# Output projection joined to the turn by quarters, and the low parts of its first weights moved into the turn

## The reference

```python
mixed = jnp.concatenate([out_a, out_b], axis=-1)     # 256 tokens x 1024 features
return mixed @ w_out                                 # 1024 x 1024
# then x = x + norm(...) or x = x + gate * (...), and a feed-forward block or a mixture of experts follows
```

## Time and profile before

| | |
|---|---|
| time, median of 3 runs | 2291.13 us (2288.84 to 2291.92) |
| the profiled execution | 2288.96 us, span 2287.2 us |
| PE busy | 2098.6 us, 92% of the span |
| DVE busy | 1351.0 us, 59% |
| ACT busy | 1133.3 us, 50% |
| mean granted PE clock | 0.946 of 2.4 GHz |

### The profile page before, as it was taken

How to read it: one execution, slowest core, us unless ns; L and a number is a source line. 1 busy time by engine, 2 the same in 40 slices (tenths; PEclk the granted TensorE clock), 3 DMA queues, 4 the chain that set the end, 5 groups by cost and what they waited for, 6 DMA issues and landing times.

```text
span 2287.2 us, 31360 instructions
## 1 busy us (share of the span) xinstructions
PE 2098.6 (92%) x13218; PEld 1826.9 (80%) x13218; DVE 1351.0 (59%) x1302; ACT 1133.3 (50%) x1455; POOL 443.4 (19%) x305
## 2 busy tenths in 40 slices
PE   7998977999899899699999877999998986999997
PEld 6898967999899898699988666777777875877775
DVE  5766436556656584655653656566665247565665
ACT  4765445565566354456533534554443244454553
POOL 2683000474176100037510000000000000000000
PEclk9999988999999899799999988999998787999999
DMA  9897514787688463378754105878886203688874
GB/s 326 289 313 234 173 56 146 241 284 242 219 287 277 148 172 124 117 245 279 260 172 151 52 11 201 295 284 323 330 303 211 88 1 147 239 314 313 322 291 177
DMA packets 224348, 494.95 MB, mean 216 GB/s; under 512 B 11848, under 2 KB 167608, under 8 KB 199472
## 3 DMA queue, kind: packets, MB, share of 16 engines
q1 hardware_dynamic: 200608, 410.20, 52.3%
q0 software_dynamic: 23328, 81.71, 10.5%
q10 hardware_dynamic: 272, 1.05, 0.1%
HBM read 485.53 MB, written 12.10 MB: 218 GB/s over the span
## 4 chain that ended last, share of the span: by engine, by line
PE 82%; DVE 9%; ACT 3%; DMA 3%; issue 2%; POOL 0%; DVEq 0%; SPq 0%; ACTq 0%
PE psum L997 80%; DVE nrm L2069 2%; DMA big<-in_ada_w 2%; DVE low L2069 1%; DMA ring<-in_ffn_w_up 1%; PE psum L1063 1%; PE psum L1596 1%; ACT wh L1685 1%; PE psum L1240 1%; DVE xl L2069 1%; DVE wide L2069 0%; DMA ring<-in_moe_w_gate 0%; DVE nrm L2189 0%; DVE x L2392 0%; DVE nrm L2163 0%
## 5 line engine op out<-in xcount | busy, mean ns | idle before, releaser
L2069 DVE TENSOR_TENSOR low<-ring,wh 128x2048 fp32r<-128x2048 f32 (+2 forms) x338 | 811.3, 2416 | 532.0 <-ACT wh L1685 530.7
L1685 ACT ACTIVATE wh<-ring 128x2048 fp32r<-128x2048 f32 (+2 forms) x338 | 640.6, 1902 | 436.9 <-PE psum L997 236.8
L997 PE MATMUL psum<-xh,wh 128*128 128x256 f32 x1832 | 520.7, 284 | 13.4 <-DVE xl L2069 7.2
L997 PE MATMUL psum<-xl,wh 128*128 128x256 f32 x1832 | 520.0, 284 | 0.0
L997 PE MATMUL psum<-xh,low 128*128 128x256 f32 x1832 | 517.7, 283 | 0.0
L997 PEld LDWEIGHTS psum<-xh,wh 128*128 128x128 f32 x1832 | 352.1, 192 | 19.2 <-issue 15.5
L997 PEld LDWEIGHTS psum<-xl,wh 128*128 128x128 f32 x1832 | 350.1, 191 | 1.4
L997 PEld LDWEIGHTS psum<-xh,low 128*128 128x128 f32 x1832 | 350.5, 191 | 0.0
L769 POOL TENSOR_TENSOR big<-big 128x1024 f32<-128x1024 f32 x144 | 302.7, 2102 | 241.3 <-ACT big L1781 233.3
L997 PE MATMUL psum<-wh,xh 128*128 128x256 f32 (+5 forms) x864 | 278.6, 322 | 10.4 <-DVEq L667 5.9
L997 PE MATMUL psum<-wh,xl 128*128 128x256 f32 (+5 forms) x864 | 277.7, 321 | 0.0
(11 more groups left out here) (350 smaller groups left out, 2389.3 us busy)
## 6 DMA issues: line engine op xcount, KB each, us to landing
ring<-in_moe_w_gate SPq DMA_DIRECT2D x64, 1024.0 KB, 5.4
ring<-in_moe_w_up SPq DMA_DIRECT2D x64, 1024.0 KB, 6.0
ring<-in_moe_w_down SPq DMA_DIRECT2D x64, 1024.0 KB, 5.4
big<-in_ada_w POOLq DMA_DIRECT2D x48, 1024.0 KB, 6.7
ring<-in_ffn_w_gate SPq DMA_DIRECT2D x44, 1024.0 KB, 6.2
ring<-in_ffn_w_up SPq DMA_DIRECT2D x44, 1024.0 KB, 5.9
ring<-in_ffn_w_down SPq DMA_DIRECT2D x44, 1024.0 KB, 5.2
ring<-in_mlstm_w_in SPq DMA_DIRECT2D x16, 1024.0 KB, 5.6
```

Source lines behind the costliest of these rows:

```text
L997: return pe.matmul(out_, lhsT, rhs, start=start, stop=stop, **kw)
L1685: act.activation(wh[n % PARTS][:, 0:w], ring[SLOT_OF[n]][:, 0:w], ACT.Copy).then_inc(high, 1)
L2069: return dve.tensor_tensor(out_, a, b, op)
```

## The change

Outproj is joined to the turn ahead of it: the boundary between them is gone on all three engines. In its place PE waits, in the first piece alone, ahead of each run of 12 matmuls for the quarter of `xl` that it reads. On DVE the early low parts leave the mixer. One of them stands at the head of the turn, ahead of the four subtractions of `xl`; the second, where there was one, is made in outproj, behind the four. The high parts stay where they were.

```diff
@@ JOINED
-                                                         ("ffn", "setup"),
+                                                         ("ffn", "setup"), ("outproj", "turn"),
@@ PE, outproj
                     for t in range(TT):
                         for kt in range(KT):
+                            if j == 0 and kt % 4 == 0:
+                                pe.wait_ge(turn_low, 4 * ran(s, "turn") - 4 + 2 * t + kt // 4 + 1)
                             last = three(psum[:, 2 * t + j // 2, (j % 2) * 256:(j % 2 + 1) * 256],
@@ DVE, turn
                 if by_columns(s - 1):
                     return turn_columns(s, k)
+                if STAGES[s + 1][0] == "outproj" and early(s + 1):
+                    low_part(s + 1, PIECE0[s + 1], GU)
                 for q in range(4):
@@ DVE, outproj
             def outproj(s, k):
-                for j in range(len(early(s)), 4):
+                for j in range(min(1, len(early(s))), 4):
                     low_part(s, PIECE0[s] + j, GU)
@@ DVE, soft_attention
                     if i + 2 < len(run):
                         biased_scores(*run[i + 2])
-                    if i == len(run) - 1:
-                        for j, shape in enumerate(early(s + 2)):
-                            low_part(s + 2, PIECE0[s + 2] + j, shape)
                     if p == SOFT[name]["pairs"] - 1:
                         scaled_values(name)
@@ DVE, mlstm
-                for j, shape in enumerate(early(s + 2)):
-                    low_part(s, PIECE0[s] + j, shape)
                 dve.wait_ge(ml_act, 2 * H)
```

## The result

The changed kernel took 2277.05 us in the median of six runs (2273.09 to 2283.62), the kernel before 2290.25 (2280.44 to 2294.06). The ratio is 0.9945, with a 95% interval of 0.9926 to 0.9963: 0.55% faster, 13 us. Two later series of the same kernel gave 0.9921 (0.9905 to 0.9938) and 0.9943 (0.9924 to 0.9961), so some 15 us over the three. The prediction was 2274, with 2268 to 2283 as its range.

A forecast was written before the change was run, and what follows sets the result against it. PE, with 82% of the chain, was taken to bound the kernel. Mixer ends 8.2, boundary 6.1 and clock 3.0 us sum to 17.3, which from the 2291.13 us median gives 2274 us, rounded (range 2268 to 2283).

The forecast's parts named there:

- Low parts out of the mixer's end: At the four mixer ends, taking DVE's low parts away gives back 0.8, 2.35, 2.05 and 3.05 us, together 8.2.
- The low part inside the turn: At the turn's head, in DVE's idle time, it costs DVE's last result nothing; without that cover, 2.28 us a place.
- The boundary: Between turn and outproj, PE's first product starts right behind its transposes, needing only the first quarter: 6.1 us (5.6 to 6.6).
- The thin margin: In outproj, the second piece's low part is ready only 0.5 us before PE wants it, at one place 0.7.
- The clock: In outproj, unbroken work from the transposes on raises PE's clock sooner: +3 us of the 6.0 lost there.
- I see nothing that takes it back: In the stages behind outproj, joined and bound by PE, nothing takes back the 17.3 us gain.
- the waiting terms: At mixer ends and turns, the gains from shorter waits, 8.2 and 6.1 us, together 14.3.
- the waits go, the clock stays as it is: Rival, chance 0.27: in outproj the clock does not improve, only 14.3 us come back, time 2277 (2274 to 2280).
- The slower rival: Rival, chance 0.03: PE stays at 1.2 GHz through outproj; all four places slow to the end give 2315.

The follow-up runs named there:

- the single wait: Changed kernel with PE waiting once, ahead of its first product, for all four quarters, still without the boundary; 0.9931 and 0.9940 against the kernel before.
- the move alone: Kernel before with low parts moved as in the change, boundary between turn and outproj kept, no waits for quarters; 0.9965 and 0.9978 against the kernel before.

## Why the prediction was right, point by point

**Low parts out of the mixer's end: right.** 0.8, 2.35, 2.05 and 3.05 us were forecast. The three traces gave 0.69; 2.33, 2.35 and 2.29; 1.99, 1.84 and 1.99; and 2.98: 7.9 to 8.0 us for 8.2. What is late next was also as named: at A, C and D PE's last products, 0.1 us ahead of DVE's first write, and at B ACT's squares.

**The low part inside the turn: right,** and now shown from both sides: one at the head costs nothing, one without cover costs 4 us, and two at the head cost 2. The 2.28 us that were forecast for a lost cover were too few: they count from the fourth `xl`, which PE no longer waits for.

**The boundary: right in kind, mis-sized.** The term was 6.1 us with 6.6 as its upper end; it measured 7.1. I took PE to begin its products near the modelled end of its transposes, T0 + 3.6; it begins them at T0 + 3.14 to 3.33, some 0.3 us ahead of that end, right behind the start of the last one. The crossing itself costs next to nothing: with one wait for all quarters and no boundary the first product stands at 5.18, with the boundary at 5.13. The thin margin held: at C the second piece's low part ends at T0 + 8.2 and PE comes to that piece at T0 + 9.0, at A it is 8.4 and 9.2.

**The clock: right at the places, wrong beyond them.** I took +3 of 6.0 us. Outproj got 4.3 to 4.8 us shorter. Transposes alone bring the clock back: with the single wait no product had run before T0 + 5, and outproj at B stood at 2.4 GHz from its first product, in this trace:

```profile
930.40:953.00 22.60, 22.52 (x191) 22.55 (x192) 12.33 (x6) 8.15 (x8) 0.00 (x0) 1.00 0.44 140
```

Before, with the same 5.1 us, B had 0.92, and in the kernel with the move alone it had 0.87:

```profile
934.10:957.10 23.00, 22.96 (x171) 22.96 (x172) 11.28 (x5) 7.74 (x6) 0.00 (x0) 0.87 0.37 111
```

So an early start is not what decides. The fall ahead of the turn lay elsewhere, 6.0 us ahead of T0 in the first and 2.4 in the second, but that does not settle it: before, at B, it lay 8.3 us ahead and the clock came back only 8.8 us behind T0. What decides is not shown. The rule of the Trainium skill (TensorE: Matmul & The Clock Gate, Part 4: PE-mode transpose), by which transposes don't count towards the full clock, does not hold for the float32 transposes of this kernel: in both traces with one wait the clock rose 3.3 to 4.3 us behind T0 at all four places, ahead of the first product.

**"I see nothing that takes it back": this step failed.** I had looked only at waits. The next stages are bound by PE, and PE's speed there depends on the clock, which at A and B had fallen in the norm ahead of the ffn. The changed kernel reaches them sooner and finds it low for longer: 2.0 to 2.1 us at A in three traces, 1.9 twice at B. That is most of why 17.3 us were forecast, 19.8 seen at the places, and 13 to 18 measured.

The whole span says the same. All kernels have the same matmuls in the same order, so what differs in PE's busy time is nearly all the clock's, and the rest of the span is PE's waiting (us, from each trace's page):

| | before | changed, three | one wait, two | move alone, two |
|---|---|---|---|---|
| PE busy | 2098.6 | 2099.5, 2102.7, 2099.2 | 2095.3, 2088.4 | 2110.6, 2108.5 |
| rest of the span | 188.6 | 175.1, 173.4, 173.3 | 180.8, 182.6 | 178.2, 177.4 |

The waits gave back 13.5 to 15.3 us, where 14.3 were forecast. PE's busy time should have fallen by 3.0 and rose by 0.6 to 4.1 against the one trace of before. So the waiting terms were right in sum, and the clock's term had the wrong sign or was nothing over the program. That the time still fell near 2274 is in part luck: the places gave 2.5 us more than forecast, and the stages between took back more than that. The rival "the waits go, the clock stays as it is", 2277, names the time that came, but for another reason: the clock did help in outproj and hurt in the stages behind.

**The slower rival** did not come up: no matmul of the first piece starts more than 0.4 us behind the one ahead of it, so the waits for quarters were satisfied before PE reached them, and no outproj stayed at half clock for more than 1.4 us of products in any trace of the changed kernel.

What stays open: why C to D differs by up to 5 us between traces of one kernel, and what sets where the clock's falls and rises lie. The kernel with the move alone and the one with the single wait differ by 8 to 9 us in time, with turns and idle times alike to 0.2 us at each place. The table says what kind of time it is: PE waits 3 to 5 us less in the move alone and is busy 13 to 22 us longer with the same matmuls, so it is the clock. It is so in the other executions too: the mean granted clock is 0.944 over 23 of the move alone and 0.950 over 12 of the single wait. Why a boundary that does not lengthen the turn does this is not shown.

## What to carry to other kernels

Sum a gain on PE in two columns: what waits give, and what the clock makes of it, in the next dense stages too. A start made 1.9 us earlier four times over showed no gain in time here (within some 3 us), while an end made earlier, by taking work off the engine that PE waits for, came through: 5 to 8 us with the boundary, 14 to 16 with the single wait. The difference between these two is the clock's, so a gain of less than 10 us in this program says little about the place that was edited until PE's busy and waiting time are read apart. When an operation moves late, look at what was early only for its sake: the high parts on ACT had stood ahead of the last exponentials to feed those low parts, and moving them too gave another 9 us in the series that had both.

## What the runs showed of the hardware that was not expected

There are 44 turns joined to their outproj in the traces. In four the clock stood at 2.4 GHz from T0 on. In 36 of the other 40 it returned to 2.4 GHz 2.8 to 4.8 us behind the first transpose, with only transposes run since T0 in the kernels that waited for all quarters; in the last four it took 5.2 to 8.2 us. Where it lay was not scattered at random: at B the rise came 4.32, 4.36 and 4.24 us behind T0 in the three traces of the changed kernel, and in the ffn behind A it rose 41.07, 41.25 and 41.10 us behind T0. With the single wait, an edit that only delays PE in the turn, the same rises came 37.86 and 37.77 us behind the T0 of A. An edit thus moved the slow stretches of a later stage by some 3.3 us, and in the same way in each trace. That does not hold at every place: at C the changed kernel's rise came at 3.10, 4.71 and 3.10 us.
